# A two-layer FFN / attention-mixer / FFN kernel: bias mask per head, an earlier weight split, an earlier table load, transposes between products, and up weights stored by block

## The chip, the cores and the metric

One core of a Trainium2 chip runs the whole program. The metric is the device time of one execution in microseconds (us); lower is better. PE is TensorE (a matmul and its weight load are two records, PE and PEld), DVE is VectorE, ACT is ScalarE, POOL is GpSimd and SP is SyncE, which here only issues DMAs.

## The reference

`x` is 256 x 1024 in fp32 and goes through two layers. Each has a feed-forward part, a mixer and a second feed-forward part, each on the RMS-normed input and added to `x`:

```
x = x + 0.5 * swiglu(rms_norm(x, ffn1_norm[l]), ffn1_w_up[l], ffn1_w_down[l])
x = x + hybrid_mixer(rms_norm(x, mix_norm[l]), w_in[l], na_rel_bias[l], w_branch_a[l], w_branch_b[l], w_out[l], pos)
x = x + 0.5 * swiglu(rms_norm(x, ffn2_norm[l]), ffn2_w_up[l], ffn2_w_down[l])
```

`swiglu` is `(silu(gate) * up) @ w_down`, with `w_up` 1024 x 5632 and `w_down` 2816 x 1024. The mixer projects to q, k, v of 12 dilated-window heads and 8 neighbourhood heads and to two gates of 1024, runs both attentions (rotary positions on the dilated heads, a relative bias and a column mask on the neighbourhood heads), multiplies by two branch weights, gates, adds, and multiplies by `w_out`.

## The kernel before, in words

**Weights.** All weights stream through three slots in units of 128 x 2048 fp32 (1 MB), 96 units per layer: 33 of the first FFN, 30 of the mixer (from `M_AT`), 33 of the second FFN. SP issues two DMAs per unit into `raw[slot]` as soon as DVE has done the lower split of the unit that was there (`lo_done`). Products are in fp32r with an upper and a lower part of each operand, three products for one. ACT copies `raw` to `w_hi` (`hi`, L533) once the DMA has landed and PE has freed the slot's last unit (`split_free`); DVE then subtracts into `w_lo` (`lo`, L756); PE waits for `lo_done`. ACT, DVE and PE each run their instructions strictly in the order in which the code lists them, so this order is a schedule written by hand.

**FFN.** 11 chunks of 256 hidden columns; each takes a unit of gate weights (U), one of up weights (V) and one of down weights. In `up` (L1131 to L1134) the weights are the stationary operand, tiles of 128 x 128 (512 bytes per partition), and `a_both`, the transposed input, both parts side by side, is the moving one. For each of two column blocks b and eight k it issues a 512-column product with `w_hi` and a 256-column product with `w_lo`, a pair; the two blocks write two PSUM banks. In `w_hi` and `w_lo` the tile of k and b lies at `k * FC + b * P`, as in `raw`, so tiles of neighbouring k are 1024 bytes apart. The lines are

```
at = k * FC + b * P
w = w_hi[slot][:, at:at + P]
mm = pe.matmul(pair[:, b, 0:SEQ], w_lo[slot][:, at:at + P], a_hi[:, k, :], start=False, stop=False)
```

Then ACT and DVE gate: `u_lower` (ACT L591), `u_half` (DVE L830 frees U's banks by `u_read`, L834 scales by the row factors of L610), `tanh` (ACT L602), `gate` (DVE L840), `v_lower` (ACT L598), `v_half` (DVE L845 frees V's banks by `v_read`, L848 makes hT), `hT_upper` (ACT L606) and `hT_lower` (DVE L852). PE multiplies hT by the down unit (`rows`, L1069 to L1071). In chunk 0 the splits of units 3 and 4, `hi` and `lo`, stand behind `v_lower` and `v_half`. At the end of an FFN, ACT splits the next stage's first unit (`next_hi`) between `v_lower` and `hT_upper`, and PE's last products wait for `hT_lower` of chunk 10.

**Input of a stage.** DVE adds the accumulators to `x` in four groups (L768), PE transposes each group (`input_transposes`, L1107), ACT scales and rounds it into the upper part (L541), DVE makes the lower part (L781). In the mixer's first two units (`input_products`) PE runs, for each half a of the contraction and each row tile t, a `part` of four k's, 12 products of 512 columns; behind each of the two parts of a = 0 come the transposes of group 2, then of group 3. `part(1, 1)` needs the lower part of group 3.

**Mixer.** Steps m = 0 to 29 take one unit each. ACT's `hi` for step m + 2 waits until the unit of step m - 1 is freed. In steps 2, 4 and 6 DVE runs a `rope` (L886 four times, L889 twice) behind its split, and PE transposes its result (L1243) in the middle of a later unit. From step 9 on, `masked` (L921) adds masks or bias to the scores.

**Bias.** POOL's queue spreads the relative bias in DRAM by 24 DMAs during the first FFN; SP loads it into `bias` (128 x 8 heads x 6 x 64) at each layer's first FFN's end. POOL then adds the column mask to all of it in one instruction (L493) and, behind it, computes the mixer's norm factors (L466 to L474). DVE waits for `bias_ready` at pair 6, step 16.

**Start.** ACT issues its DMAs and waits for `gainT_ready`; its first activation, and with it the load of the function table, comes after. SP loads units 0 and 1 in halves (`first_part`), ACT and DVE split them in halves (`first_hi` L712, `first_lo` L1044).

Of the kernel before, what the change touches and what calls it, by code (L numbers as in the profile page):

```python
# [6 lines left out]
ALU = mybir.AluOpType  # L7
# [96 lines left out]
def build(nc, x_in, gains, w_up, w_down, w_in, rel_bias, w_a, w_b, w_out, consts, out):  # L104

    bias_rows = nc.dram_tensor("bias_rows", [DEPTH, P, NA_HEADS, BIAS_ROWS, GRID_W], F32, kind="Internal").ap()
    with ExitStack() as ctx:
# [38 lines left out]
        wait_carrier = sb("wait_carrier", [P, 1])  # L146
        credits = sb("credits", [P, 2 * RING])
        cst = sb("cst", [P, C_ALL])
# [120 lines left out]
        result_ready = sem("result_ready")  # L269
        out_written = sem("out_written")  # L270

        GROUP4 = ((0, 0), (1, 0), (0, 1), (1, 1))
# [187 lines left out]
        def _(pool):  # L460
# [28 lines left out]
            for l in range(DEPTH):  # L489

                pool.wait_ge(bias_loaded, l * 16 + 16)
                rows = bias[:, :, :, :].rearrange("p h r k -> p (h r) k")
                pool.tensor_tensor(rows, rows, na_mask.unsqueeze(1).to_broadcast([P, NA_HEADS * BIAS_ROWS, GRID_W]),  # L493
                                   ALU.add).then_inc(bias_ready, 1)
                norm_factors(l * PHASES + 1)

                pool.wait_ge(mix_ready, l + 1)
                pool.wait_ge(o_read, l * PAIRS + DIL_PAIRS)
                oh = o_dil[:, :, :, :].rearrange("p h t d -> p (h t) d")
                wts = mix_d[:, :, :].rearrange("p g j -> p (g j)").unsqueeze(2).to_broadcast([P, DIL_HEADS * TT, HD])  # L500
                pool.tensor_tensor(oh, oh, wts, ALU.mult).then_inc(mix_part, 1)
                pool.wait_ge(mix_part, l * 2 + 1)
                og = [o_dil[:, g * GROUP_HEADS:(g + 1) * GROUP_HEADS, :, :] for g in range(GROUPS)]
                pool.tensor_tensor(og[0], og[0], og[1], ALU.add).then_inc(mix_part, 1)
                pool.wait_ge(mix_part, l * 2 + 2)
                ya = y[:, :, 0:GROUP_HEADS * HD].rearrange("p t (h d) -> p h t d", h=GROUP_HEADS)
                pool.tensor_tensor(ya, og[0], og[2], ALU.add).then_inc(y_dil_done, 1)
                norm_factors(l * PHASES + 2)
                if l < DEPTH - 1:
                    norm_factors(l * PHASES + 3)  # L510
# [6 lines left out]
        def _(act):  # L517
# [5 lines left out]
            def hi(l, at, u, c=None):  # L523
# [8 lines left out]
                act.wait_ge(split_free, n + 1)  # L532
                act.activation(w_hi[slot][:, :], raw[slot][:, :], ACT.Copy).then_inc(hi_done, 1)  # L533

# [43 lines left out]
            def feed_forward(l, f, at):  # L578
# [28 lines left out]

                u_lower(0)
                act.wait_ge(rows_turned, ff + 1)
                act.activation(half_rstd_rows, bank[ROWS][:, 0:SEQ], ACT.Copy).then_inc(rows_ready, 1)  # L610
                tanh(0)
                v_lower(0)
                hi(l, at, 3)
                hi(l, at, 4)
# [94 lines left out]
            def first_hi(a, h):  # L709

                act.wait_ge(part_arrived[2 * a + h], 32)
                half = act.activation(w_hi[a][:, h * D:(h + 1) * D], raw[a][:, h * D:(h + 1) * D], ACT.Copy)  # L712
                half.then_inc(part_hi if h == 0 else hi_done, 1)

            act.wait_ge(gainT_ready, 1)
            transposed_hi(0, 0)
# [26 lines left out]
        def _(dve):  # L743
# [5 lines left out]
            def lo(l, at, u, c=None):  # L749
# [3 lines left out]
                if c is not None:  # L753
                    n = n + c * 3
                dve.wait_ge(hi_done, n + 1)
                dve.tensor_tensor(w_lo[slot][:, :], raw[slot][:, :], w_hi[slot][:, :].bitcast(F32),  # L756
                                  ALU.subtract).then_inc(lo_done, 1)

# [61 lines left out]
            def feed_forward(l, f, at):  # L820
# [5 lines left out]
                def u_half(c):  # L826
# [4 lines left out]
                    dve.wait_ge(u_read, n)  # L831
                    if isinstance(c, int) and c == 0:
                        dve.wait_ge(rows_ready, ff + 1)
# [23 lines left out]
                v_half(0)  # L857
                lo(l, at, 3)
                lo(l, at, 4)
# [125 lines left out]
            def mixer(l):  # L985
# [3 lines left out]
                for m in range(M_UNITS):  # L989
                    p = step_pair(m)  # L990
                    before = step_pair(m - 1)
                    for hh in range(2):
                        if before is not None:
                            probs_turned(l, 2 * before + hh)
                        if p is not None:
                            if p == DIL_PAIRS and hh == 0:
                                dve.wait_ge(bias_ready, l + 1)
                            masked(l, 2 * p + hh)
# [38 lines left out]
            def first_lo(a, h):  # L1037

                part = slice(h * D, (h + 1) * D)
                if h == 0:  # L1040
                    dve.wait_ge(part_hi, a + 1)
                else:
                    dve.wait_ge(hi_done, a + 1)
                half = dve.tensor_tensor(w_lo[a][:, part], raw[a][:, part], w_hi[a][:, part].bitcast(F32), ALU.subtract)  # L1044
                half.then_inc(part_lo if h == 0 else lo_done, 1)
# [20 lines left out]
        def _(pe):  # L1066
# [43 lines left out]
            def input_products(l, ph, at, part):  # L1110


                for a in range(2):
                    split_ready(l, at, a)
                    for t in range(TT):
                        pe.wait_ge(xT_lo, ph * 4 + 2 * a + t + 1)
                        part(a, t)
                        if a == 0:
                            input_transposes(ph, t + 2)

            def up(slot, pair, ks, between=None):

                for b in range(2):
                    if b == 1 and between is not None:
                        between()
                    for k in ks:
                        at = k * FC + b * P
                        w = w_hi[slot][:, at:at + P]
# [155 lines left out]
            def mixer(l):  # L1284
                ph = l * PHASES + 1
                def first_chunk(a, t):
                    mm = cols((M_AT + a) % RING, t, a, bank[PROJ[0][t]], a == 0, a == 1)
                    if t == 1:
# [176 lines left out]
```

## Time and profile before

| | us |
|---|---|
| median of 3 runs | 1189.33 (1189.02 to 1190.08) |
| the profiled execution | 1190.21 |
| its span | 1188.4 |
| PE busy | 1166.5 (98%) |
| DVE busy | 792.4 (67%) |
| ACT busy | 589.0 (50%) |
| POOL busy | 59.7 (5%) |
| mean granted clock of PE | 0.993 |

Busy times are sums over instructions; matmuls overlap, so PE's is an upper bound. In a timeline, a row has its start and its length in us, and in brackets how long the engine stood idle before it and who released it. Several instructions of one kind are merged into one row (x2, x4). The granted clock is 1.00 at 2.4 GHz and 0.50 at 1.2 GHz. Times count from the start of the span.

### The profile page before, as it was taken

The page shows a single profiled execution, that of the slowest core. Times are in us where ns is not written, and L with a number is a line of the kernel's source. Part 1 is how long each engine was busy: PE and PEld are TensorE (multiplying, and loading weights), DVE is VectorE, ACT ScalarE, POOL GpSimd, SP SyncE. Part 2 cuts the span into 40 slices and gives each one's busy share as a digit, 9 for nine tenths or more (in the row PEclk, how much of TensorE's full clock was granted, in tenths as well). Part 3 has the DMA queues.
Part 4 walks back from the last instruction along what each step waited for, and adds up shares of the span by engine and source line. Part 5 has one row for each costly group of instructions (what it writes and reads, how often), then busy time and mean ns, then how long its engine had stood idle before and what let it go on. Part 6 is the DMA issues. An engine that isn't in the chain of part 4 may idle for free.

```text
span 1188.4 us, 16054 instructions
## 1 busy us (share of the span) xinstructions
PE 1166.5 (98%) x6163; PEld 982.0 (83%) x6163; DVE 792.4 (67%) x992; ACT 589.0 (50%) x771; POOL 59.7 (5%) x70
## 2 busy tenths in 40 slices
PE   8999998999999999999999999999999999999997
PEld 6888886888888888888888888878888888888886
DVE  5766667755675776666686667777557567766665
ACT  6444443655544464444474454455555436544443
POOL 0011112000200000000000000200002000000000
PEclk9999998999999999999999999999999999999999
DMA  8666655653334455555556555645434435655551
GB/s 267 223 221 215 214 188 195 198 170 129 125 125 177 142 205 184 185 203 178 178 179 208 180 192 194 229 142 189 165 108 142 153 140 179 211 184 192 196 178 35
DMA packets 145601, 211.54 MB, mean 178 GB/s; under 512 B 7648, under 2 KB 112272, under 8 KB 145296
## 3 DMA queue, kind: packets, MB, share of 16 engines
q1 hardware_dynamic: 142960, 206.33, 50.9%
q0 software_dynamic: 1920, 3.20, 0.8%
q10 hardware_dynamic: 672, 1.37, 0.4%
q8 instruction: 29, 0.48, 0.2%
q14 instruction: 20, 0.16, 0.0%
HBM read 209.77 MB, written 4.19 MB: 180 GB/s over the span
## 4 chain that ended last, share of the span: by engine, by line
PE 93%; DVE 5%; ACT 1%; issue 1%; POOLq 0%; POOL 0%; DVEq 0%; ACTq 0%
PE banks L1134 23%; PE banks L1069 16%; PE banks L1071 15%; PE banks L1070 15%; PE banks L1132 13%; PE banks L1131 3%; PE banks L1280 2%; PE banks L1253 2%; PE banks L1265 1%; DVE w_lo L756 1%; PE banks L1107 1%; ACT w_hi L533 1%; PE banks L1243 1%; DVE gates L840 1%; DVE hT_lo L852 1%
## 5 line engine op out<-in xcount | busy, mean ns | idle before, releaser
L756 DVE TENSOR_TENSOR w_lo<-raw,w_hi 128x2048 fp32r<-128x2048 f32 x190 | 434.7, 2290 | 184.3 <-ACT w_hi L533 184.2
L533 ACT ACTIVATE w_hi<-raw 128x2048 fp32r<-128x2048 f32 x190 | 363.0, 1914 | 238.1 <-PE banks L1071 235.7
L1134 PE MATMUL banks<-a_both,w_hi 128*128 128x512 f32 x1232 | 439.5, 396 | 0.0
L1132 PE MATMUL banks<-a_both,w_lo 128*128 128x256 f32 x1408 | 364.3, 279 | 0.0
L1132 PEld LDWEIGHTS banks<-a_both,w_lo 128*128 128x128 f32 x1408 | 265.4, 189 | 14.7
L1134 PEld LDWEIGHTS banks<-a_both,w_hi 128*128 128x128 f32 x1232 | 231.2, 188 | 47.5
L1069 PE MATMUL banks<-w_hi,a_both 128*128 128x512 f32 (+1 forms) x448 | 181.6, 405 | 1.3 <-DVE a_both L781 0.9
L1071 PE MATMUL banks<-w_hi,a_both 128*128 128x512 f32 (+1 forms) x448 | 172.1, 384 | 0.0
L1070 PE MATMUL banks<-w_lo,a_both 128*128 128x512 f32 (+1 forms) x448 | 171.5, 383 | 0.0
L1069 PE MATMUL banks<-w_hi,hT_hi 128*128 128x512 f32 x320 | 125.0, 391 | 0.5 <-DVE hT_lo L852 0.5
L1071 PE MATMUL banks<-w_hi,hT_lo 128*128 128x512 f32 x320 | 124.5, 389 | 0.0
L1070 PE MATMUL banks<-w_lo,hT_hi 128*128 128x512 f32 x320 | 124.5, 389 | 0.0
L1069 PEld LDWEIGHTS banks<-w_hi,a_both 128*128 128x128 f32 x448 | 84.4, 188 | 20.6 <-issue 4.0
L1071 PEld LDWEIGHTS banks<-w_hi,a_both 128*128 128x128 f32 x448 | 84.2, 188 | 17.4
L1070 PEld LDWEIGHTS banks<-w_lo,a_both 128*128 128x128 f32 x448 | 84.6, 189 | 12.9
L591 ACT ACTIVATE gates<-banks 128x512 f32<-128x512 f32 x44 | 26.3, 597 | 120.6 <-PE banks L1134 120.6
L598 ACT ACTIVATE gates<-banks 128x512 f32<-128x512 f32 x44 | 26.2, 596 | 100.6 <-PE banks L1134 100.6
L1131 PE MATMUL banks<-a_both,w_hi 128*128 128x512 f32 x176 | 70.2, 399 | 2.0 <-DVE a_both L781 1.1
L1071 PEld LDWEIGHTS banks<-w_hi,hT_lo 128*128 128x128 f32 x320 | 60.1, 188 | 12.7
L1070 PEld LDWEIGHTS banks<-w_lo,hT_hi 128*128 128x128 f32 x320 | 60.1, 188 | 12.6
L1069 PEld LDWEIGHTS banks<-w_hi,hT_hi 128*128 128x128 f32 x320 | 60.1, 188 | 11.7 <-issue 0.8
L830 DVE TENSOR_TENSOR gates<-banks,gates 128x512 f32<-128x512 f32 x44 | 30.5, 692 | 46.9 <-ACT gates L591 46.9
(104 smaller groups left out, 1014.7 us busy)
## 6 DMA issues: line engine op xcount, KB each, us to landing
raw<-ffn_w_up_dram SPq DMA_DIRECT2D x172, 512.0 KB, 4.2
raw<-w_in_dram SPq DMA_DIRECT2D x92, 512.0 KB, 4.4
raw<-ffn_w_down_dram SPq DMA_DIRECT2D x88, 512.0 KB, 3.9
raw<-w_out_dram SPq DMA_DIRECT2D x16, 512.0 KB, 4.1
raw<-w_branch_b_dram SPq DMA_DIRECT2D x8, 512.0 KB, 4.1
bias_rows<-na_rel_bias_dram POOLq DMA_DIRECT2D x24, 128.0 KB, 4.4
bias<-bias_rows SPq DMA_DIRECT2D x2, 1536.0 KB, 7.2
raw<-ffn_w_up_dram SPq DMA_DIRECT2D x8, 256.0 KB, 5.6
```

Of the source, the lines that this page charges most:

```text
L533: act.activation(w_hi[slot][:, :], raw[slot][:, :], ACT.Copy).then_inc(hi_done, 1)
L591: act.activation(u_low, U_BANKS[:, :, SEQ:2 * SEQ], ACT.Copy).then_inc(u_low_done, 1)
L598: act.activation(v_low, V_BANKS[:, :, SEQ:2 * SEQ], ACT.Copy).then_inc(v_low_done, 1)
L756: dve.tensor_tensor(w_lo[slot][:, :], raw[slot][:, :], w_hi[slot][:, :].bitcast(F32), ALU.subtract).then_inc(lo_done, 1)
L830: dve.tensor_tensor(u_sum, U_BANKS[:, :, 0:SEQ], u_low, ALU.add).then_inc(u_read, 1)
L1069: pe.matmul(dst, s_hi, m_hi, start=start, stop=False)
L1070: pe.matmul(dst, s_hi, m_lo, start=False, stop=False)
L1071: return pe.matmul(dst, s_lo, m_hi, start=False, stop=stop)
L1131: mm = pe.matmul(pair[:, b, :], w, both, start=True, stop=False)
L1132: mm = pe.matmul(pair[:, b, 0:SEQ], w_lo[slot][:, at:at + P], a_hi[:, k, :], start=False, stop=False)
L1134: mm = pe.matmul(pair[:, b, :], w, both, start=False, stop=k == KT - 1)
L1253: mm = pe.matmul(bank[SC[hh]][:, t * SEQ:t * SEQ + keys(h)], qT[rows_, p, t * P:(t + 1) * P], kT[rows_, p, k0:k0 + keys(h)], start=True, s ...
```

## The change

- `by_block`: the splits of all U and V units write `w_hi` and `w_lo` in the order b, k, n, reading `raw` in runs of 128 elements; down and mixer units stay as they are. `up` reads the tile at `b * KT * P + k * P`: neighbouring k are 512 bytes apart.
- POOL computes the mixer's norm factors first, then adds the mask to one head at a time (128 x 384), head h after the unit of mixer step 3 + h is freed. `bias_ready` counts eight per layer.
- In chunk 0 of each FFN, ACT splits unit 3 right behind `u_lower` (ahead of the row factors and the tanh), DVE between the two instructions of `u_half`.
- ACT copies one element of `warm` into an added column of `credits` before its first wait for `gainT_ready`.
- In the mixer's input products each part of four k's is issued in two halves; the transposes of groups 2 and 3 come between the halves of the parts of a = 0.

```diff
 wait_carrier = sb("wait_carrier", [P, 1])
-credits = sb("credits", [P, 2 * RING])
+credits = sb("credits", [P, 2 * RING + 1])
 cst = sb("cst", [P, C_ALL])
...
+def by_block(split, place, unit, k0=0, k1=KT):
+    src = place[:, :].rearrange("p (k b n) -> p b k n", b=2, n=P)
+    dst = split[:, :].rearrange("p (b k n) -> p b k n", b=2, n=P)
+    q = unit % L_UNITS
+    q = q if q < F_UNITS else q - F2_AT
+    if q in (0, 1) or 0 < q < F_UNITS - 1 and q % 3 != 1:
+        return dst[:, :, k0:k1, :], src[:, :, k0:k1, :]
+    return split[:, :], place[:, :]
 GROUP4 = ((0, 0), (1, 0), (0, 1), (1, 1))
...
         pool.wait_ge(bias_loaded, l * 16 + 16)
-        rows = bias[:, :, :, :].rearrange("p h r k -> p (h r) k")
-        pool.tensor_tensor(rows, rows, na_mask.unsqueeze(1).to_broadcast([P, NA_HEADS * BIAS_ROWS, GRID_W]),
-                           ALU.add).then_inc(bias_ready, 1)
         norm_factors(l * PHASES + 1)
+        for h in range(NA_HEADS):
+            pool.wait_ge(split_free, RING + l * L_UNITS + M_AT + 4 + h)
+            pool.tensor_tensor(bias[:, h, :, :], bias[:, h, :, :],
+                               na_mask.unsqueeze(1).to_broadcast([P, BIAS_ROWS, GRID_W]),
+                               ALU.add).then_inc(bias_ready, 1)
...
         act.wait_ge(split_free, n + 1)
-        act.activation(w_hi[slot][:, :], raw[slot][:, :], ACT.Copy).then_inc(hi_done, 1)
+        dst, src = by_block(w_hi[slot], raw[slot], at + u + (c or 0) * 3)
+        act.activation(dst, src, ACT.Copy).then_inc(hi_done, 1)
...
         u_lower(0)
+        hi(l, at, 3)
         act.wait_ge(rows_turned, ff + 1)
...
         v_lower(0)
-        hi(l, at, 3)
         hi(l, at, 4)
...
         act.wait_ge(part_arrived[2 * a + h], 32)
-        half = act.activation(w_hi[a][:, h * D:(h + 1) * D], raw[a][:, h * D:(h + 1) * D], ACT.Copy)
+        half = act.activation(*by_block(w_hi[a], raw[a], a, 4 * h, 4 * h + 4), ACT.Copy)
         half.then_inc(part_hi if h == 0 else hi_done, 1)
+    act.wait_ge(warm_set, 1)
+    act.activation(credits[:, 2 * RING:2 * RING + 1], warm[:, 0:1], ACT.Copy)
     act.wait_ge(gainT_ready, 1)
...
         dve.wait_ge(hi_done, n + 1)
-        dve.tensor_tensor(w_lo[slot][:, :], raw[slot][:, :], w_hi[slot][:, :].bitcast(F32),
-                          ALU.subtract).then_inc(lo_done, 1)
+        dst, src = by_block(w_lo[slot], raw[slot], at + u + (c or 0) * 3)
+        upper, _ = by_block(w_hi[slot], raw[slot], at + u + (c or 0) * 3)
+        dve.tensor_tensor(dst, src, upper.bitcast(F32), ALU.subtract).then_inc(lo_done, 1)
...
             dve.wait_ge(u_read, n)
-            if isinstance(c, int) and c == 0:
+            if c == 0:
+                lo(l, at, 3)
                 dve.wait_ge(rows_ready, ff + 1)
...
         v_half(0)
-        lo(l, at, 3)
         lo(l, at, 4)
...
                     if p == DIL_PAIRS and hh == 0:
-                        dve.wait_ge(bias_ready, l + 1)
+                        dve.wait_ge(bias_ready, (l + 1) * NA_HEADS)
                     masked(l, 2 * p + hh)
...
-        part = slice(h * D, (h + 1) * D)
         if h == 0:
...
             dve.wait_ge(hi_done, a + 1)
-        half = dve.tensor_tensor(w_lo[a][:, part], raw[a][:, part], w_hi[a][:, part].bitcast(F32), ALU.subtract)
+        dst, src = by_block(w_lo[a], raw[a], a, 4 * h, 4 * h + 4)
+        upper, _ = by_block(w_hi[a], raw[a], a, 4 * h, 4 * h + 4)
+        half = dve.tensor_tensor(dst, src, upper.bitcast(F32), ALU.subtract)
         half.then_inc(part_lo if h == 0 else lo_done, 1)
...
                 pe.wait_ge(xT_lo, ph * 4 + 2 * a + t + 1)
-                part(a, t)
+                part(a, t, (0, 1))
                 if a == 0:
                     input_transposes(ph, t + 2)
+                part(a, t, (2, 3))
...
             for k in ks:
-                at = k * FC + b * P
+                at = b * KT * P + k * P
                 w = w_hi[slot][:, at:at + P]
...
         ph = l * PHASES + 1
-        def first_chunk(a, t):
-            mm = cols((M_AT + a) % RING, t, a, bank[PROJ[0][t]], a == 0, a == 1)
+        def first_chunk(a, t, js):
+            mm = cols((M_AT + a) % RING, t, a, bank[PROJ[0][t]], a == 0, a == 1, js)
+            if js[-1] < 3:
+                return
             if t == 1:
...
```

## Rows read from the trace of the kernel before

**Rows 1.** the page's busy times: us (share of the span) xinstructions

```profile
PE 1166.5 (98%) x6163; PEld 982.0 (83%) x6163; DVE 792.4 (67%) x992; ACT 589.0 (50%) x771; POOL 59.7 (5%) x70
```

**Rows 2.** timelines of SP and ACT near the start: start us, us, engine, line

```profile
5.99 1.28 ACT L541 ACT_TABLE_LOAD   x1 [5.99 <-PE banks L1107]
...
16.66 0.93 SPq L331 DMA_DIRECT2D raw<-ffn_w_up_dram  x2
```

**Rows 3.** DMA issues of the first 30 us: KB each, median us to landing

```profile
raw<-ffn_w_up_dram SPq DMA_DIRECT2D x6, 512.0 KB, 5.9
```

**Rows 4.** timelines of ACT, DVE and PE from 24 to 31 us

```profile
25.39 0.63 ACT L602 ACTIVATE gates<-gates 128x512 f32<-128x512 f32 x1 [0.83 <-DVE gates L834]
...
28.35 4.50 DVE L756 TENSOR_TENSOR w_lo<-raw,w_hi 128x2048 fp32r<-128x2048 f32 x2 [0.27 <-ACT w_hi L533]
...
30.69 0.50 PE L1131 MATMUL banks<-a_both,w_hi 128*128 128x512 f32 x1 [0.91 <-DVE w_lo L756]
```

**Rows 5.** timelines of POOL, DVE, ACT and PE, end of layer 0's first FFN

```profile
185.19 6.82 POOL L493 TENSOR_TENSOR bias<-bias,cst 128x3072 f32<-128x3072 f32 x1 [9.08 <-DMA bias<-bias_rows]
...
185.28 7.27 DVE L840 SCALAR_TENSOR_TENSOR gates<-gates 128x512 f32<-128x512 f32 x1
...
189.21 1.92 ACT L533 ACTIVATE w_hi<-raw 128x2048 fp32r<-128x2048 f32 x1 [2.39 <-DMA raw<-w_in_dram]
...
193.91 0.63 ACT L606 ACTIVATE yT_hi<-probsT 128x512 fp32r<-128x512 f32 x1 [2.78 <-DVE probsT L848]
...
189.88 0.39 PE L1071 MATMUL banks<-w_hi,hT_lo 128*128 128x512 f32 x1
...
195.41 0.77 PE L1069 MATMUL banks<-w_hi,yT_hi 128*128 128x512 f32 x1 [5.14 <-DVE yT_lo L852]
```

**Rows 6.** stages: busy us of each engine, then PEclk, DMA share, GB/s

```profile
193.28:200.11 6.83, 4.70 (x11) 3.77 (x12) 4.24 (x4) 1.35 (x3) 0.00 (x0) 0.50 0.21 64
...
780.37:783.79 3.42, 3.42 (x11) 2.64 (x10) 1.71 (x3) 0.72 (x2) 0.00 (x0) 0.50 0.40 110
```

**Rows 7.** timelines of POOL, DVE and PE, end of layer 1's first FFN

```profile
763.22 8.36 POOL L493 TENSOR_TENSOR bias<-bias,cst 128x3072 f32<-128x3072 f32 x1 [157.35 <-DMA bias<-bias_rows]
...
764.80 7.33 DVE L852 TENSOR_TENSOR hT_lo<-probsT,hT_hi 128x512 fp32r<-128x512 f32 x1
...
772.27 0.47 PE L1069 MATMUL banks<-w_hi,hT_hi 128*128 128x512 f32 x1 [0.55 <-DVE hT_lo L852]
...
779.12 0.47 PE L1069 MATMUL banks<-w_hi,yT_hi 128*128 128x512 f32 x1 [2.49 <-DVE yT_lo L852]
```

**Rows 8.** timelines of ACT and PE, start of layer 0's mixer

```profile
208.80 1.14 ACT L541 ACTIVATE a_both<-banks,gainT 128x128 fp32r<-128x128 f32 x4 [2.36 <-PE banks L1107]
...
215.16 0.50 PE L1069 MATMUL banks<-w_hi,a_both 128*128 128x512 f32 x1 [0.44 <-DVE a_both L781]
```

**Rows 9.** timelines of DVE, ACT and PE's weight loads around the second rotation

```profile
232.12 2.29 DVE L756 TENSOR_TENSOR w_lo<-raw,w_hi 128x2048 fp32r<-128x2048 f32 x1 [3.74 <-ACT w_hi L533]
...
234.32 2.50 DVE L886 TENSOR_TENSOR gates<-qk_raw,cst 128x512 f32<-128x512 f32 x4
...
235.61 1.92 ACT L533 ACTIVATE w_hi<-raw 128x2048 fp32r<-128x2048 f32 x1 [2.37 <-PE banks L1071]
...
238.08 0.85 PEld L1243 LDWEIGHTS banks<-cst,gates 128*128 128x128 f32 x8 [0.27 <-DVE gates L889]
```

**Rows 10.** timeline of PE, up products: block starts, then two neighbouring pairs

```profile
27.61 0.40 PE L1134 MATMUL banks<-a_both,w_hi 128*128 128x512 f32 x1
...
27.97 0.40 PE L1134 MATMUL banks<-a_both,w_hi 128*128 128x512 f32 x1
...
180.43 0.39 PE L1131 MATMUL banks<-a_both,w_hi 128*128 128x512 f32 x1
...
183.25 0.40 PE L1131 MATMUL banks<-a_both,w_hi 128*128 128x512 f32 x1
...
186.02 0.39 PE L1069 MATMUL banks<-w_hi,hT_hi 128*128 128x512 f32 x1
```

## The prediction, made blind

> **What bounds the kernel now.** I read the page's busy times first: TensorE (PE) is busy for 98% of the span [rows 1]. So time can only be won where PE stands still, where its clock is low, or where its products follow each other more slowly than they could. The timeline of PE, read with those of DVE, ACT and POOL at its few holes, gives the list; in the rows the reader is to see how far the start lies behind the row before it, and who released it. A product of 512 columns takes 0.227 us from start to start where nothing disturbs it (the 18 of a down product run from 186.02 to 189.88, 17 steps) [rows 5, 10]; a hole costs what the row calls idle plus about 0.16 us, since 195.41 less 190.11, where the next product was due, is 5.30 where the row says 5.14.
>
> The holes are: 30.69, waiting for a split of a V block in the first FFN [rows 4]; 195.41, the end of layer 0's first FFN, 5.30 us [rows 5]; 772.27 and 779.12, the same place in layer 1, 0.71 and 2.65 us [rows 7]; 215.16, in the mixer's first product, 0.60 us, with a twin in layer 1 [rows 8]. After both FFN ends the granted clock is 0.50, the lower of its two levels, 1.2 GHz: for 6.83 us in layer 0, of which PE worked 4.70, and 3.42 us in layer 1, all worked [rows 6]. Work at half speed loses half its time: 2.35 and 1.7 us.
>
> The cause of the two big holes is one instruction. POOL adds the mask to all eight heads' bias, 6.82 us, and a DVE instruction beside it that takes 0.69 us elsewhere takes 7.27 [rows 5] and 7.33 us [rows 7]. In layer 1 POOL's own row shows 8.36 us: it was ready at 763.22, but got on only as DVE's product ended at 764.8. So the two exclude each other, the one that runs ends first, and POOL is served before the next of DVE.
>
> **Mask per head, removed from the FFN's end.** Layer 1: both holes go, 0.71 + 2.65, and with them the cause of the low clock, 1.7: 5.1 us. Layer 0: the hole does not close, because what is late next is a transfer. ACT splits the mixer's first weights only at 189.21, when their DMA lands, and `hT_upper` stands behind that split on ACT [rows 5]. The split ends at 191.1; from ACT's upper part of hT to PE's start it was 195.41 - 193.91 = 1.50 us; so PE starts at 192.6, 2.8 us sooner than 195.41, and a hole of 2.5 us stays. That is as long as the 2.65 of layer 1, after which the clock fell for 3.42 us; I take the same here, 1.7 us lost in place of 2.35. Layer 0: 2.8 + 2.35 - 1.7 = 3.5 (5.2 if the clock stays up). Together **-8.6 us**.
>
> **Mask per head, added to the mixer.** Eight instructions per layer of 384 elements, an eighth of 6.82, 0.85 us each. Head h waits for the same count of freed units as ACT's split in step 4 + h, so it starts when ACT starts that split. DVE then mostly waits for ACT: the row at 232.12 shows 3.74 us of idle, ACT's 1.9 us among them [rows 9], and a mask fits in. But in steps 5 and 7, heads 1 and 3, DVE is in the middle of a rotation: it runs from 234.32 (four products, then two sums, some 3.7 us), the split and so the mask start at 235.61, and PE's transposes wait for the rotation's last sum, with the weight load held for 0.27 us already [rows 9]. There is no slack: what the rotation loses PE loses. The loss of DVE in rows 5 is 7.27 - 0.69 = 6.58, 0.24 less than the mask's 6.82, so a mask of 0.85 to 1.05 (a fixed start of its own counted) costs 0.6 to 0.8; I take 0.8. Two per layer, two layers: **+3.2 us**. Ends: 0 if POOL slips between, 4.2 with 1.05 in full. The norm factors are now ahead of the masks on POOL, which waits for nothing in them longer than before. Behind masks 5 to 7 the scoring of the first pairs begins on DVE; the Trainium skill, "SBUF — State Buffer", section "Who interferes with whom", says that a DVE instruction with at most one SBUF input is not held by GpSimd, which by that page prices those three at nothing. Without that page their other end is 3 x 0.8 x 2 = 4.8 us more; I take nothing, as most of them fall where DVE waits.
>
> **Second split ahead of the gating.** ACT and DVE split unit 3 before the first chunk's tanh and products, in all four FFNs. In the first one PE's V block at 30.69 waited for DVE's split, which stood behind the whole gating [rows 4]. Moved, it is bound by its transfer: the second of the two DMAs is issued at about 17.1 [rows 2] and lands 5.9 later [rows 3], 23.0; ACT 1.92, DVE 2.29: 27.25. But the gating now comes behind it: product 0.69, tanh 0.63, product 0.69, V sum 0.69, 29.9, and PE may write the V banks only after that sum. New start 30.0: **-0.7 us** (0.3 to 1.1 as the landing varies). In the other three there is no hole to win, and the lengthened chain must not make one: from U's last product 0.6 + 1.92 + 2.29 + 0.69 + 0.63 + 0.69 + 0.69 = 7.5 us, against 8 pairs of V and 16 of U, 24 x 0.35 = 8.4. It fits, with 0.9 to spare.
>
> **Table at once.** The table load of 1.28 us goes ahead of the wait at 5.99 [rows 2]. It is ahead of PE's first product, but what follows hangs on DMAs: unit 3's landing, worked out above, does not move, and the hole at 30.0 takes up whatever PE gained before. Nothing; at best 1.3. The added copy of one element is hidden by ACT's idle 5.99 us; the longer `credits` tile may move the constants behind it by 4 bytes, which I price at nothing.
>
> **Transposes within products.** PE issues the transposes of groups 2 and 3 after half of a 12-matmul part, 6 x 0.227 = 1.4 us sooner. ACT idles 2.36 before it turns to group 2 at 208.80 [rows 8], x is updated by then, and ACT's and DVE's pieces behind it move up by the same 1.4, more than the 0.60 us of hole at 215.16. The count of transposes is unchanged. Two layers: **-1.2 us**.
>
> **Up weights by block.** ACT and DVE now read raw in runs of 128 elements; both have idle time per chunk, and I price it at nothing (cover: PE is the bound; if they became slower by a third the splits would come late). On PE a stationary tile lies 512 bytes from the last, not 1024. Up products come in pairs (512 and 256 columns) that should take 1.5 x 0.227 = 0.340, but a block of eight takes 2.82 (180.43 to 183.25) or 2.77 (to 186.02) [rows 10], 0.352 and 0.346 a pair, and the slowest neighbours are 0.36 apart (27.61, 27.97). The two blocks differ in nothing but the tile's place, by 512 bytes, and the PSUM bank. So place may matter, and no row shows which way. The bounds for 1408 pairs, at (2.82 + 2.77) / 16 = 0.3494 now: 0.340 gives -13.2, 0.36 gives +15; all like the faster block -4.4, all like the slower one +4.4. New blocks mix both places, so I take **0**. The Trainium skill, "SBUF — State Buffer", section "Who interferes with whom", says that PE has two independent read ports, for moving operand and weight load, and never waits on anyone; by that page this part is 0 and the sum stands, by the fast end of the rows it would be 13 us better.
>
> **Sum.** -8.6 + 3.2 - 0.7 - 1.2 = -7.3 us. The profiled execution took 1190.21 us (span 1188.4 and 1.8 around it), 0.9 above the median of 1189.33. 1190.2 - 7.3 = 1182.9 against its own time, 1182.1 against the median.
>
> **Rivals.**
> - The tile's place matters much: pairs go toward 0.340. For it: the page's 98% hides a pitch above 0.340 in all 1408 pairs; against it: no row with the new distance. Half of the gain gives 1175, all of it 1169. Chance 0.20.
> - The masks do not touch the rotations. For it: 0.85 us is short; against it: both rows of the trace show POOL served right after the DVE instruction that ran. 1182.1 - 3.2 = 1179. Chance 0.12.
> - The other side: 512 bytes is the bad distance, all pairs go to 0.36. 1182.1 + 15 = 1197; it makes the kernel slower from a pitch of 0.3494 + 7.3/1408, or 0.355, on. For it: 0.36 does occur; against it: never in a whole block. Chance 0.12, half of it past no change.
> - The change doesn't remove the FFN-end holes: the mask leaves, but the split's DMA holds layer 0 as before, or DVE's order lets a new wait in, at V's banks in three FFNs. It gives back 3 to 5: 1187. Chance 0.06.
> - My forecast, 0.50.
>
> **Numbers.** A measurement of this kernel can tell about 0.2%, 2.4 us, from no change. Faster takes the forecast, the first two rivals and a part of the others: 0.84; within 0.2% 0.10; slower 0.06. The range reaches from three quarters of the fast pitch, 1171, to half of the slow one, 1189. The forecast's own range is 1178 to 1186.
>
> **What would show it.** Right: no POOL row beside the FFN end in layer 1, no idle row and clock 1.00 there; in layer 0 a hole of 2.5 us released from ACT behind the DMA; rotations in steps 5 and 7 near 4.5 us, with PE's weight loads waiting 0.8 for them; no hole near 215; a V start at 30.0. For the layout, the starts of the up blocks: 2.77 to 2.82 apart. Wrong: block starts at 2.72 or 2.88, or ACT's and DVE's splits above 1.92 and 2.29 us.

## The result, and the profile after

The changed kernel takes a median of 1180.24 us (1179.60 to 1180.81, four runs) against 1189.51 for the kernel before on the same chip: a ratio of 0.9922, 95% interval 0.9905 to 0.9939. It is faster by 9.3 us, where 7.3 were forecast. The profiled execution took 1180.81 us, its span 1179.0, against 1190.21 and 1188.4.

The page of the changed kernel, busy times, answers to [rows 1]; the two groups below it are the two splits, with their mean durations (1914 and 2290 ns), which the new reading order leaves as they were. Line numbers are higher by 12 to 18 than before.

```profile
PE 1163.2 (99%) x6163; PEld 980.4 (83%) x6163; DVE 781.6 (66%) x992; ACT 588.4 (50%) x772; POOL 62.5 (5%) x84
...
L773 DVE TENSOR_TENSOR w_lo<-raw,w_hi 128x2048 fp32r<-128x2048 f32 x190 | 434.9, 2290 | 188.8 <-ACT w_hi L546 188.8
L546 ACT ACTIVATE w_hi<-raw 128x2048 fp32r<-128x2048 f32 x190 | 363.4, 1914 | 240.8 <-PE banks L1088 237.0
```

PE has 6163 products before and after, so the lead of the new kernel can be read product by product: the start of the n-th product before, less the start of the n-th after. Read where the order of the products is the same in both, it is a ledger of every hole:

| stretch | lead gained (us) | forecast |
|---|---|---|
| start to the V block at 30 | 0.75 | 0.7 |
| end of layer 0's first FFN | 5.12 | 3.5 (5.2 if the clock stays up) |
| hole in the mixer's first product, two layers | 1.50 | 1.2 |
| rotations with a mask, two layers | -3.33 | -3.2 |
| end of layer 1's first FFN | 5.16 | 5.1 |
| all the rest of 1179 us | 0.15 | 0 |

Together 9.35, and the spans differ by 9.4. The mixer's hole is worth 0.75 us in each layer and not 0.60, because the first product behind a hole takes longer too: from 215.16 in [rows 8] to the next it is 0.33 us, where 0.227 is usual.

**The FFN ends.** ACT, DVE and PE at the end of layer 0's first FFN, from the three engines' timelines, against [rows 5]:

```profile
188.40 1.91 ACT L546 ACTIVATE w_hi<-raw 128x2048 fp32r<-128x2048 f32 x1 [2.33 <-DMA raw<-w_in_dram]
190.22 0.61 ACT L619 ACTIVATE yT_hi<-probsT 128x512 fp32r<-128x512 f32 x1
...
190.86 0.69 DVE L869 TENSOR_TENSOR yT_lo<-probsT,yT_hi 128x512 fp32r<-128x512 f32 x1 [3.35 <-ACT yT_hi L619]
...
191.70 0.47 PE L1086 MATMUL banks<-w_hi,yT_hi 128*128 128x512 f32 x1 [2.19 <-DVE yT_lo L869]
```

DVE's short operation `yT_lo` takes 0.69 us; before, one short operation of DVE took 7.27 in layer 0 and one 7.33 in layer 1. Late now is the transfer, and ACT's upper part stands behind the split that waits for it. The hole is 2.35 us, for 2.5 forecast. The stretches around both FFN ends, with the same columns as [rows 6], show the granted clock at 1.00:

```profile
189.00:201.00 12.00, 9.81 (x48) 7.70 (x47) 8.24 (x15) 7.25 (x15) 0.00 (x0) 1.00 0.52 174
770.00:785.00 15.00, 15.00 (x76) 12.28 (x75) 12.45 (x20) 9.84 (x23) 0.00 (x0) 1.00 0.39 123
```

**The rotations.** POOL, DVE and PE's weight loads around the first rotation that has a mask beside it, against [rows 9]:

```profile
229.01 1.51 POOL L505 TENSOR_TENSOR bias<-bias,cst 128x384 f32<-128x384 f32 x1 [4.42 <-PE banks L1088]
236.26 1.01 POOL L505 TENSOR_TENSOR bias<-bias,cst 128x384 f32<-128x384 f32 x1 [5.74 <-PE banks L1088]
...
227.74 3.32 DVE L902 TENSOR_TENSOR gates<-qk_raw,cst 128x512 f32<-128x512 f32 x4
230.99 1.28 DVE L905 TENSOR_TENSOR gates<-gates 128x512 f32<-128x512 f32 x2
...
232.32 0.31 PEld L1261 LDWEIGHTS banks<-cst,gates 128*128 128x128 f32 x3 [1.10 <-DVE gates L905]
```

The mask takes 1.01 us where DVE is idle and 1.51 where it first has to wait. The four products take 3.32 us instead of 2.50, and PE's weight load idles 1.10 instead of 0.27: 0.83 lost, straight to PE. PE's start after it lies 0.84 late, and so do those at 245.02, 811.01 and 823.70.

**The first V block and the up blocks.** PE, against [rows 4] and [rows 10]:

```profile
29.99 0.47 PE L1149 MATMUL banks<-a_both,w_hi 128*128 128x512 f32 x1 [0.56 <-DVE gates L862]
...
176.90 0.40 PE L1149 MATMUL banks<-a_both,w_hi 128*128 128x512 f32 x1
179.68 0.39 PE L1149 MATMUL banks<-a_both,w_hi 128*128 128x512 f32 x1
182.49 0.40 PE L1149 MATMUL banks<-a_both,w_hi 128*128 128x512 f32 x1
```

V starts at 29.99, released by the V sum (30.0 and that sum were forecast). Up blocks lie 2.78 and 2.81 us apart, as before.

### The profile page after: what moved, and what is told of

It reads as the page before. It is cut to its first block, busy times and chain, and to the rows that moved or that the text cites. A ratio compares the mean times of both kernels' runs of the same rounds, so it can differ in the third digit from the quotient of the medians.

```text
span 1179.0 us, 16070 instructions
## 1 busy us (share of the span) xinstructions
PE 1163.2 (99%) x6163; PEld 980.4 (83%) x6163; DVE 781.6 (66%) x992; ACT 588.4 (50%) x772; POOL 62.5 (5%) x84
## 4 chain that ended last, share of the span: by engine, by line
PE 91%; DVE 4%; DMA 2%; ACT 2%; issue 1%; SPq 0%; POOLq 0%; POOL 0%; DVEq 0%; ACTq 0%
PE banks L1152 23%; PE banks L1086 15%; PE banks L1088 15%; PE banks L1087 15%; PE banks L1150 13%; PE banks L1149 3%; PE banks L1298 2%; PE banks L1271 2%; PE banks L1283 1%; ACT w_hi L546 1%; DVE gates L902 1%; DMA raw<-ffn_w_up_dram 1%; PE banks L1261 1%; DMA raw<-w_in_dram 1%; PE banks L1124 1%
## 5 line engine op out<-in xcount | busy, mean ns | idle before, releaser
L773 DVE TENSOR_TENSOR w_lo<-raw,w_hi 128x2048 fp32r<-128x2048 f32 x190 | 434.9, 2290 | 188.8 <-ACT w_hi L546 188.8
L546 ACT ACTIVATE w_hi<-raw 128x2048 fp32r<-128x2048 f32 x190 | 363.4, 1914 | 240.8 <-PE banks L1088 237.0
```

The source lines that it names most:

```text
L546: act.activation(dst, src, ACT.Copy).then_inc(hi_done, 1)
L773: dve.tensor_tensor(dst, src, upper.bitcast(F32), ALU.subtract).then_inc(lo_done, 1)
```

## The experiments

Each difference is against the kernel before in the runs with "alone" in their names, and otherwise against the changed kernel. A hole is given as its cost: distance of two starts, less the pitch. Kernels with a ratio were timed in rounds against the kernel before; those without have one time, beside before's median of the same chip.

**1. The layout alone.**

```
-                at = k * FC + b * P
+                at = b * KT * P + k * P
(and by_block in ACT's and DVE's splits)
```

> The kernel before with only the up weights stored by block. Theory (the tile's place is nothing to PE): 1189.5 us within 0.1%, and the starts of the up blocks 2.82 and 2.77 us apart in turn, as before; ACT's split 1.91 and DVE's 2.29 us although raw is read in runs of 128. Rival (the place matters and the whole change hid a gain behind a loss): block starts other than these, and a time off by 88 blocks of U and V pairs, 2 x 88 x 0.05 us = 9 us for each 0.05 us a block.

Measured: 1189.33 us, ratio 0.9999, 0.9989 to 1.0009 (ten runs against thirteen). Up blocks are as before, the splits too. The layout is worth nothing within 0.1%. The profiled execution was 1.5 us shorter than that of before, all of it from one place: after the hole of 2.66 us at 779.19 the clock stayed up. The stretches behind that hole in the kernel before stand in [rows 6]; here, window 770 to 790:

```profile
770.00:790.00 20.00, 16.95 (x81) 13.47 (x80) 17.35 (x22) 8.96 (x17) 1.65 (x1) 1.00 0.34 107
```

So the clock after such a hole does not follow from the hole's place and length alone; this matters below. The kernel before varies too: over its 13 timed runs on this chip the mean granted clock was 0.991 to 0.996 and the time 1192.04 to 1187.83.

**2. The mask per head alone.**

```
-                pool.tensor_tensor(rows, rows, na_mask...).then_inc(bias_ready, 1)
+                for h in range(NA_HEADS):
+                    pool.wait_ge(split_free, RING + l * L_UNITS + M_AT + 4 + h)
+                    pool.tensor_tensor(bias[:, h, :, :], ...).then_inc(bias_ready, 1)
```

> The kernel before with only the mask per head behind the norm factors. Theory: the two holes at the FFN ends go except for the 2.4 us in layer 0 that the DMA of the mixer's first weights holds, no stretch at clock 0.50 but the end, and four new holes of 0.84 us at the transposes behind the second and third rotations: 1189.5 - (5.3 - 2.4 + 2.35) - (0.7 + 2.65 + 1.7) + 3.4 = 1182.6 us. Rival 1 (the low clock stays after the 2.4 us hole): 1184.3. Rival 2 (the new holes come from something else of the change, such as the block layout): 1179.2 and no holes at the rotations.

Measured: 1182.10 us, ratio 0.9934 (0.9917 to 0.9950). It carries most of the change. The profile has the hole at 192.88, 2.58 us, released by DVE's `yT_lo` behind the DMA, nothing at layer 1's FFN end, and four rotation holes of 0.84. The clock fell at 194.18 for 3.41 us, as the forecast had assumed; in the profile of the whole change it did not. That profiled execution (1185.19 us) is the slowest of the four by 2.9, and its span is 5.0 shorter than that of before, where the medians differ by 7.3.

**3. The second split alone.**

```
+                hi(l, at, 3)      (ACT: ahead of the row factors and tanh(0))
-                hi(l, at, 3)      (ACT: behind v_lower(0)); the same for DVE's lo
```

> The kernel before with only the second split ahead of the gating. Theory: the hole at 30.69 becomes one released by DVE's V sum (L845's work) instead of by a split, PE starts near 30.0, 0.7 us sooner; no hole of over 0.13 us in chunk 0 or 1 of the other three FFNs. Rival: the gating, now late, makes holes in those FFNs, and the gain of 0.7 is lost.

Measured once: 1189.59 us beside 1189.35. V now waits for DVE's V sum, as worked out, and no other FFN has a hole. But unit 3 landed at 24.0, not 23.0, and V started at 31.08, no sooner than the 30.69 of before. The gain isn't there in this execution.

**4. The table load alone.**

```
+            act.wait_ge(warm_set, 1)
+            act.activation(credits[:, 2 * RING:2 * RING + 1], warm[:, 0:1], ACT.Copy)
```

> The kernel before with only the early table load. Theory: ACT's first copy starts 1.3 us sooner, at 6.0, but PE's first product only about 0.4 us sooner, at 11.6, since ACT's split of the first half unit still waits for its DMA to about 8.2; the V start behind the first chunk then moves from 30.69 by the same 0.4 at most. Rival: PE's first product moves by the whole 1.3.

Measured once: 1191.67 us beside 1189.35. ACT's first copy moved from 7.28 to 6.22, but PE's warm-up products, which take 0.427 us at 1.2 GHz and 0.216 at 2.4, ran at the lower level until 13.3 us, where before they were fast from 5.6 on. V started at 32.36. The slow start covers the term: inconclusive on it, and no sign of a gain. The changed kernel has the same early load and was at the lower level until about 10.2 in its profile; its first product began at 11.60, for 11.98 before.

**5. The transposes alone.**

```
-                part(a, t)
+                part(a, t, (0, 1))
                 if a == 0:
                     input_transposes(ph, t + 2)
+                part(a, t, (2, 3))
```

> The kernel before with only the transposes between halves of a part. Theory: the holes of 0.60 us near 215 and 798 go and nothing else moves; 1.2 us, 0.1%, too little to see in one time. Rival (they go only because the mask left DVE free): they stay, as the mask is still in its old place here.

Measured once: 1186.41 us beside 1188.30. The holes of 0.60 near 215 and 798 are gone, in a trace that keeps the others (the one at the end of layer 0's first FFN is 4.56 us here for 5.30), with the mask still in its old place. This term is shown in the trace.

**6. Masks moved off the rotations.**

```
-    pool.wait_ge(split_free, RING + l * L_UNITS + M_AT + 4 + h)
+    pool.wait_ge(split_free, RING + l * L_UNITS + M_AT + (4, 6, 8, 9, 10, 11, 12, 13)[h])
```

> The changed kernel with the eight masks moved to steps 4, 6, 8, 9, 10, 11, 12 and 13, so that none starts beside a rotation. Theory (POOL's lock on DVE makes the four holes of 0.84 us): no holes at the transposes behind rotations, 1180.2 - 3.4 = 1176.9 us; heads 4 to 7 now run beside the scoring, whose DVE instructions read one operand from SBUF and are not held. Rival 1 (the rotation is late for another reason): the holes stay, 1180.2. Rival 2 (the scoring is held too): new holes of up to 0.9 us in steps 10 to 13, and the gain falls to nothing.

Measured: 1177.66 us, ratio 0.9909 (0.9888 to 0.9929). All four rotation holes are gone. Timelines of POOL and DVE around the same rotation:

```profile
224.41 1.01 POOL L505 TENSOR_TENSOR bias<-bias,cst 128x384 f32<-128x384 f32 x1 [14.40 <-PE banks L1088]
236.27 1.01 POOL L505 TENSOR_TENSOR bias<-bias,cst 128x384 f32<-128x384 f32 x1 [10.84 <-PE banks L1088]
...
228.59 2.50 DVE L902 TENSOR_TENSOR gates<-qk_raw,cst 128x512 f32<-128x512 f32 x4
```

With no mask between 225.42 and 236.27 the products are back at 2.50 us. The cause of the 3.3 us in the ledger is the mask beside the rotation, and nothing else. Four masks now stand beside the scoring, in steps 10 to 13, and no hole appears there. It is the trace that shows this: the times alone, 0.9909 against 0.9922 with intervals of 0.002 to either side, don't separate this kernel from the changed one.

**7. One undivided mask at step 8.**

```
-    for h in range(NA_HEADS):  wait ... M_AT + 4 + h;  mask of head h
+    pool.wait_ge(split_free, RING + l * L_UNITS + M_AT + 8)
+    pool.tensor_tensor(rows, rows, na_mask...).then_inc(bias_ready, 1)
```

> The changed kernel with the mask again in one instruction of 6.8 us, but started in the mixer's step 8, clear of the rotations. It asks whether the gain came from the cut into heads or from the place. Theory (the place: DVE's next split, due two steps later, is held for 5 us and still in time): no hole at the FFN ends and none at the rotations, at most 0.5 us in steps 9 and 10, 1177 us, as with the masks clear. Rival (6.8 us in one piece are too long anywhere): a hole of 1 us or more in steps 9 to 11, released by the softmax or by a split.

Measured: 1178.43 us, ratio 0.9911 (0.9895 to 0.9928). POOL's mask and the DVE split beside it, from their timelines:

```profile
249.24 6.82 POOL L505 TENSOR_TENSOR bias<-bias,cst 128x3072 f32<-128x3072 f32 x1 [38.07 <-PE banks L1087]
...
251.21 7.00 DVE L772 TENSOR_TENSOR w_lo<-raw,w_hi 128x2048 fp32r<-128x2048 f32 x1 [3.74 <-ACT w_hi L545]
```

DVE's split is held for 4.7 us and PE has no hole: at this place there is that much slack. So the gain of the change came from the place of the mask and not from cutting it in eight; the cut, as placed, cost 3.3 us of it in the traces. The times (0.9911 for 0.9922) are too close to show that difference by themselves; in the profiled execution a low clock behind the hole near 192 took 1.7 us of it back.

**8. The bias transfer behind the mixer's first weights.**

```
     (SP, mixer units)
+        if m == 3:  sp.wait_ge(bias_spread, ...);  sp.dma_start(bias..., bias_rows...)
     (POOL)   norm_factors(l * PHASES + 1)  ahead of  pool.wait_ge(bias_loaded, ...)
```

> The changed kernel with SP's wait for the spread bias and its bias DMA behind the third mixer unit's DMAs, and POOL's wait for it behind the norm factors. Theory (the 2.35 us hole at 191.7 is the landing of the mixer's first weights behind the bias on SP's queue): the hole goes, 1180.2 - 2.35 = 1177.9 us, and the clock cannot fall there. Rival (DVE's or ACT's own chain holds PE there too): a hole of 0.5 us or more stays, released by ACT or DVE and not behind a DMA.

Measured: 1179.44 us, ratio 0.9920 (0.9903 to 0.9936). The hole at 191.7 is gone. ACT's timeline there:

```profile
188.47 1.91 ACT L547 ACTIVATE w_hi<-raw 128x2048 fp32r<-128x2048 f32 x1
190.28 0.62 ACT L620 ACTIVATE yT_hi<-probsT 128x512 fp32r<-128x512 f32 x1
```

The split no longer waits for a transfer, only for its turn. Against the 1177.9 of the theory the time is 1.5 too high, and the ratio is that of the change. In the profiled execution (1180.97 us) PE began its first product at 11.17, sooner than the 11.60 of the changed kernel, while unit 3 landed at 23.8, later than its 22.9. So the hole ahead of the first V block grew to 2.11 us, and the clock fell behind it for 3.4 us, which gives back 1.7. The other three executions, 1178.91 to 1179.59 us, were not profiled, so whether the same kept them above 1177.9 is not shown. PE's row, and the stretch behind it:

```profile
30.88 0.47 PE L1150 MATMUL banks<-a_both,w_hi 128*128 128x512 f32 x1 [1.94 <-DVE gates L863]
...
31.80:35.20 3.40, 3.40 (x13) 2.92 (x12) 3.40 (x3) 2.70 (x3) 0.00 (x0) 0.50 0.30 94
```

**9. Up products in groups of two.**

```
-   per k: product of 512, product of 256
+   per two k's: 512, 512, 256, 256
```

> The changed kernel with the up products in the order of two 512-column ones, then two 256-column ones (the last two k the other way round). It measures what sets the 0.3494 us of a pair. Theory (the loss comes at each change between a 512 and a 256-column product, since a block's first products, whose order differs, show 227 and 113 ns): half as many changes, blocks 0.03 to 0.06 us shorter, 88 x 2 x 0.045 = 8 us sooner, 1172. Rival (the loss comes where the next weight load, which needs up to 0.120 us where 256-column products stand in a row, is longer than the 0.1135 of the product beside it): two in a row lose as much, 1180 within 2 us or later.

Measured: 1182.52 us, ratio 0.9943 (0.9926 to 0.9960). Blocks are 2.79 to 2.81 us where they were 2.78 and 2.81, so two of them are no shorter; over the four FFNs PE falls behind by another 1.3 us in all. My theory, that a change between the two widths costs the 0.006 to 0.012 a pair, fell. Half as many changes of width gave nothing, as the rival on record had it. The starts between 40 and 175 us show where a pair's excess lies: a 512-column product holds the next for 0.234 us in the changed kernel and 0.232 here, for 0.227 in a down product; a 256-column one for 0.116 and 0.118, for 0.1135, half of that. Why both take longer in either order, by the weight loads or otherwise, is not shown.

**10. The two blocks exchanged.**

```
-                for b in range(2):
-                    if b == 1 and between is not None:
+                for b in (1, 0):
+                    if b == 0 and between is not None:
```

> The changed kernel with column block 1 before block 0 in every up unit, so that the PSUM bank and the tile's place change their turn. It asks why one block takes 2.82 and the next 2.77 us. Theory (it is the bank or the place that makes a block slow): the first block of a unit takes 2.77, the second 2.82. Rival (it is the state in which a block begins): still 2.82 first, then 2.77. The time stays within 1 us of 1180.2 in both.

Measured once: 1183.42 us beside 1188.90. PE's starts of three blocks in a row:

```profile
41.91 0.39 PE L1149 MATMUL banks<-a_both,w_hi 128*128 128x512 f32 x1
44.72 0.40 PE L1149 MATMUL banks<-a_both,w_hi 128*128 128x512 f32 x1
47.50 0.39 PE L1149 MATMUL banks<-a_both,w_hi 128*128 128x512 f32 x1
```

The first block of a unit is the long one (2.81) and the second the short one (2.78), as before the exchange. Neither the bank nor the tile's place makes the difference; what does is left open. The time is 3.2 above the 1180.2 that was expected: in its trace PE begins the first V block 0.8 later than in the changed kernel (30.79), and the clock fell near 192, which cost 1.7.

**11. V sum ahead of the gating.**

```
     (DVE, chunk 0)  u_half: ... lo(l, at, 3)
+                            v_sum(0)
                             product, [tanh], product
     (ACT)           v_lower(0) ahead of tanh(0)
```

> The changed kernel with the V sum of chunk 0 (ACT's lower half and DVE's sum, which free the V banks) right behind the second split and ahead of the row scaling, tanh and gating. In six kernels with the early second split the first FFN's V start came 7.0 to 7.1 us after the landing of unit 3's DMA: split 1.9, split 2.3, then scaling, tanh, gating and V sum, 2.8. Theory: with the V sum first, V can start 1.9 + 2.3 + 0.7 = 4.9 to 5.0 us after the landing, at about 28.8, before PE is there (29.3): no hole near 30. Rival (the wait there is for the split or the DMA itself): a hole of 0.5 us or more stays, released by a split.

Measured once: 1181.84 us beside 1188.30. The hole near 30 is gone with a landing at 23.7; DVE's timeline shows the sum directly behind the split and PE starts V at 29.59:

```profile
25.79 2.29 DVE L773 TENSOR_TENSOR w_lo<-raw,w_hi 128x2048 fp32r<-128x2048 f32 x1 [2.27 <-ACT w_hi L546]
27.99 0.68 DVE L863 TENSOR_TENSOR gates<-banks,gates 128x512 f32<-128x512 f32 x1
28.59 0.68 DVE L852 TENSOR_TENSOR gates<-gates,probsT 128x512 f32<-128x512 f32 x1
```

Its time is no better than that of the change. In the trace the clock fell for 3.41 us behind the hole of 2.11 at 191.03, 1.7 us, and that is more than the earlier V block and the shorter hole won.

**12. Runs 6, 8 and 11 together.**

> The changed kernel with masks clear of the rotations, the bias DMA behind the third mixer unit, and the V sum first. Theory: of the holes of the changed kernel none of over 0.4 us is left, -3.4 - 2.35 - 0.7 = 1173.8 us. Rival (the holes are each other's cover, or DMAs and the clock take back a part): 1176 or more.

Its edit is the sum of those three. Measured: 1174.88 us (1174.57 to 1175.32), ratio 0.9888 (0.9872 to 0.9905): the fastest version, 13.4 us under the kernel before. The theory said 1173.8, the rival 1176 and more; it lies 1.1 from either. Both were reckoned on a chip where the kernel before took 1189.51, and here it took 1188.30, so by its ratio it stands for 1176.2, where the rival begins: from 0.9922 to 0.9888 are 4.0 us, for the 6.4 of the three holes. With intervals of 0.002 to either side the times decide nothing. The profile decides for the theory, since behind the start PE has no hole above 0.24 us but two of 0.36, at 381.34 and 958.47, which every version has, and its span of 1172.8 is 6.2 shorter than the changed kernel's 1179.0. The stretch that held the two rotations of [rows 9]:

```profile
230.00:260.00 30.00, 30.00 (x170) 25.05 (x168) 16.63 (x30) 17.10 (x26) 4.01 (x4) 1.00 0.53 176
```

## Why the prediction was right

The forecast, 1182.1, missed 1180.24 by 1.9 us, and the likeliest case was the one that happened. By its own steps:

**The cause of the FFN-end holes** was read rightly: the mask instruction held DVE's short operation. Undivided but elsewhere (run 7) it leaves both places free of that hole. Layer 1 gave 5.2 for 5.1.

**Layer 0's remaining hole** was seen in advance with its size, 2.35 for 2.5, and its cause, the mixer's first transfer; run 8, which sends the bias behind three of the mixer's units, removes it. The failed step is the clause behind it, "I take the same here, 1.7 us lost": the clock stayed up in the profiled execution. The other branch, "5.2 if the clock stays up", is what the ledger shows (5.12). That is 1.6 of the 2.1 us between -7.3 and -9.4; the mixer's first product gave 0.3 more than its term, the rest 0.15. It holds for the two profiled executions. The medians differ by as much, but of the change's other three runs one has a mean granted clock of 0.996 for the profile's 0.998, and it was no slower (1180.16), so they don't bear out the clock as their reason. The clause was not a wrong reading of the row so much as one row taken for a rule, and that the clock stayed up in this profile was luck, which no row of before foretold. Over all profiles of this study, a hole of 2.1 to 2.6 us near 192 was followed by a low clock in five of seven (runs 2, 7, 9, 10, 11; not in the change or run 6), and one of 2.65 at 779 in three of five (before, runs 3 and 4; not runs 1 and 5). The length does not tell them apart: behind 2.11, 2.20 and 2.34 the clock fell, behind 2.30, 2.35 and 2.66 it did not. Two neighbours, run 7 and run 6, from 191 to 198 us:

```profile
191.00:198.00 7.00, 5.85 (x21) 4.66 (x22) 4.38 (x4) 1.81 (x7) 0.00 (x0) 0.76 0.55 170
```

```profile
191.00:198.00 7.00, 5.39 (x28) 4.45 (x29) 5.05 (x7) 2.70 (x9) 0.00 (x0) 1.00 0.53 170
```

Run 7 did 21 products in the time in which run 6 did 28, with the smaller hole. The right entry would have been 1.7 us times the eight cases of twelve, 1.1 us, with both ends in the range.

**The rotation collisions**, +3.2, were +3.3 in the ledger, at the four places named, with 0.84 for 0.8 each. Run 6 removes them and nothing else. The rival "the masks do not touch the rotations" fell.

**The scoring beside masks 5 to 7** was priced at nothing, in part by what the Trainium skill says in "SBUF — State Buffer", section "Who interferes with whom", of DVE instructions with at most one SBUF input: outside the 2-port modes they do not contend with GpSimd. The trace agrees as far as it goes: in the changed kernel two of these three masks meet a DVE instruction, a copy out of PSUM; it runs within the mask in its usual 0.69 us, and PE has no hole there. The scoring instruction itself, whose inputs are a bank of PSUM and one tile in SBUF, meets a mask in run 6: it starts at 288.53 beside the mask of 287.71 to 288.71 and takes its usual 0.29. POOL and DVE in the changed kernel:

```profile
261.47 1.00 POOL L505 TENSOR_TENSOR bias<-bias,cst 128x384 f32<-128x384 f32 x1 [5.78 <-PE banks L1088]
...
261.86 0.69 DVE L914 COPY probsT<-banks 128x512 f32<-128x512 f32 x1 [2.09 <-PE banks L1283]
```

**The second split**, -0.7, is a mis-sized term, although the profiled execution shows 0.75. The chain was right to its last step: V starts 7.0 to 7.1 us behind unit 3's landing, which is where ACT's split of it starts, in the change (22.9, 29.99) and in runs 3, 6, 7, 8, 9 and 10 (23.5 to 24.0, 30.55 to 31.08). But the landing I took, 23.0, came in only two of the nine profiles with this part (22.9 in the change, 22.8 in run 12), and in the trace of before itself that DMA landed at 23.37. The 5.9 us that I added were the median of six transfers; this one took 5.5 to 7.5 over all profiles. Later landings put the start at 30.6 to 31.1, where kernels without this part have 30.46 to 30.89 (before, runs 1, 2 and 5). Its value is about nothing on average (30.7 in the seven profiles that have it without the V sum ahead, and 30.7 in those four without it); it pays only with the V sum put ahead (run 11), which takes the gating out of the chain. ACT's rows of that split, first of the changed kernel, then of run 8:

```profile
22.94 1.91 ACT L546 ACTIVATE w_hi<-raw 128x2048 fp32r<-128x2048 f32 x1 [1.53 <-DMA raw<-ffn_w_up_dram]
```

```profile
23.83 1.92 ACT L547 ACTIVATE w_hi<-raw 128x2048 fp32r<-128x2048 f32 x1 [2.91 <-DMA raw<-ffn_w_up_dram]
```

The same instruction, from the same unit, is held 0.9 us longer by its transfer; that alone is more than the term.


**The table**, 0, can't be told from its own run (4), whose slow start covers it. PE's first product began at 11.17 to 13.33 us in the nine profiles with the early load and at 11.88 to 12.57 in the five without. **The transposes**, -1.2, are shown by run 5 and by the ledger, with 1.5: the rule of idle time and 0.16 us leaves out the slow first product behind a hole. **The layout**, 0, is shown by run 1, and both rivals with a tile's place in them, 0.32 of the chance, fell. The choice "new blocks mix both places, so I take 0" came to the right number for a wrong reason: runs 1 and 10 show no effect of the place at either distance. The Trainium skill's rule in the same section, that PE waits on no one for either port, is in agreement with the unchanged blocks. The range's lower end has a slip: 1182.1 less three quarters of 13.2 is 1172.2, not 1171; nothing hangs on it.

## What to carry to other kernels

Before you cut a long POOL instruction in pieces, look for a place where DVE, or PE behind it, has slack: an eighth in the wrong place cost 0.84 us of PE each time, the whole in the right place nothing. When the hole that you close is held by several things, name the next late one and its time, as that, and not the hole, is what the edit pays. Price a clock drop by how often it follows such a hole over several profiles, not by the one profile that you have.

## What the runs showed of the hardware

- A DVE instruction with two inputs in SBUF is held while a POOL mask runs: a rotation product loses 0.82 us to a mask of 1.01 and a split 4.7 to one of 6.82 that had begun 2.0 before it; a mask that meets a running DVE product shows 1.51 us, its own wait in it.
- A hole of 2.1 to 2.66 us was followed by 3.41 us at 1.2 GHz in 8 of 12 cases at the FFN ends and in the one case ahead of the first V block (run 8), and the same place can do both; what decides is not shown. The first rise also varied, from 4.1 us (run 3) to 13.3 (run 4), and in runs 3 and 10 the clock fell again for 3.4 us, at 7.5 and 8.6. Run 4, the latest, had its first V block 1.7 us behind that of before.
- Pairs of up products (512 and 256 columns) take 0.346 to 0.352 us where 0.340 would be their share. It isn't the tile's distance (run 1), the bank or place (run 10), or the number of changes of width (run 9); it stays open.
- The landing of the unit 3 transfer varied from 22.8 to 24.0 us in the profiles with the early split, more than the term that hung on it. It does not follow from the time of issue: its second DMA was issued at 16.4 in run 8 and landed at 23.8, and at 17.3 in run 12 and landed at 22.8.
